# Weights of a two-block transformer kernel stored word by word in pairs of chunks, so that each weight load reads every second word

## The chip, the cores and the metric

The kernel runs on one core of a Trainium2 chip. The metric is device time in microseconds from the start to the end of one execution; the median of three runs stands for a kernel. Its engines are called by the names of the profile: PE (TensorE, its matmuls), PEld (TensorE's weight loads), DVE (VectorE), ACT (ScalarE), POOL (GpSimd) and SP (SyncE, which issues the transfers).

## The reference

Two transformer blocks of two layers each work on 256 latent tokens and 256 context tokens of width 1024, in float32. The first block has window attention, a Fourier mix and a short convolution between a wide input and an output projection; the second has three parts in each layer: a SwiGLU feed-forward, a mixer (differential attention with an mLSTM in layer 0, gated linear attention in layer 1) and another feed-forward. What matters here are the dense products with weights:

```python
y = gated_merge(a, ga, f, gf, s, gc, w_out)            # h @ w_out, 1024 x 1024, inputs by h @ w_in, 1024 x 2816
...
def swiglu(h, w_in, w_out):                            # 1024 x 5632 and 2816 x 1024, four pairs of them
    a, b = jnp.split(h @ w_in, 2, axis=-1)
    return (jax.nn.silu(a) * b) @ w_out
...
px = _split(hx @ w_in, EVEN_SPLITS)                    # mixers: 1024 x 3088, 1024 x 3104, and 1024 x 1024 out
```

## The kernel before

**Units and chunks.** A weight matrix is worked through in units of 1024 rows and 128 columns. Such a unit lies in SBUF as eight chunks `c` of 128 rows (the partitions) by 128 columns, one chunk behind the other: 1024 words of 4 bytes in each partition. An output projection of a feed-forward has units of six and five chunks.

**Split.** Float32 products are made of three products of a shorter format (`F32R`). Each unit that lands by DMA in `stage`, `wgate` or `deep` is split in two tiles of the same shape: `act_split` (L1467, on ACT) writes `w_hi`, a copy rounded to the short format, and `dve_split` (L1960, on DVE) writes `w_lo = unit - w_hi`. Both tiles have `RING` = 4 slots; the split of a unit waits until the unit four before it is used up (`unit_done`), and the feed runs `LEAD` = 3 units ahead of PE. The activations are split the same way into `h_hi`, `h_lo` (normed input) or `g_hi`, `g_lo` (the gated middle of a feed-forward).

**Matmul.** For each chunk, for each of the pairs (`w_hi`, `h_hi`), (`w_hi`, `h_lo`), (`w_lo`, `h_hi`) and for each 256 tokens there is one matmul: it loads a 128x128 chunk of a weight tile into the array as the stationary operand (the profile's LDWEIGHTS, PEld) and streams 256 words of activations (MATMUL, PE). So every matmul has a weight load of its own. Of `[:, u % RING, c, :]` the load takes 128 words that lie side by side. Most of this is in `pe_gemm` (L1118); the same form stands in the first GEMMs (L863), in `cross` and `head` (L962, L993) and in `seam`, the passage between a feed-forward and the next stage (L1035, L1065). In the names of the profile `ps<-h_hi,w_hi` the streamed tile stands first and the loaded one second.

**Token-major units.** The four short GEMMs with `evac="tok"` (V of the mixers, L1162) swap the roles: the activations are loaded and the weights `w_part[wp][:, u % RING:u % RING + 2, c, :]` are streamed.

**Order.** Every engine's program is written out by hand and tied by counting semaphores. Addresses are laid out by hand too: the tiles follow each other in the order of `sizes`, in which all but one are multiples of 8 KB in a partition (`vtok`, which lies ahead of the weights, has 64 bytes over), so `h_hi`, `h_lo`, `g_hi` and `g_lo` start at one place modulo 8 KB, and `w_hi` and `w_lo` 64 bytes further.

Of the kernel before, what the change touches and what calls it, by code (L numbers as in the profile page):

```python
# [16 lines left out]
P = 128  # L17
D = 1024
KC = D // P
SEQ = 256  # L20
# [330 lines left out]
def build_program(nc, t, const, out):  # L351
# [3 lines left out]
    with ExitStack() as stack:  # L355
# [189 lines left out]
        def arrival(u, i=0, turn=0):  # L545
# [11 lines left out]
            v = u - first_deep  # L557
            return deep[:, v % DEEP], deep_full[v % DEEP], i * (16 * turn // DEEP) + (16 * (v // DEEP) + 16), DEEP

        def splits(p, i, j, rounds):  # L560

            k = p.kw
            for s in range(k["per"]):
                x = j * k["per"] + s + LEAD + k.get("ahead", 0)
                if rounds > 1 or k["fed"] or i * k["step"] * k["per"] + x < k["n"] * k["per"]:
                    yield x
# [263 lines left out]
        def pe_first(eng, p):  # L830

            eng.wait_ge(S("s_ready"), 2)
            w_part, x_part = {"hi": w_hi, "lo": w_lo}, {"hi": h_hi, "lo": h_lo}

            def rows(n):
                eng.wait_ge(first_full[n], 16)
                if n >= 2:
                    eng.wait_ge(S("mod_sum"), n - 1)
                for k in range(KC):
                    j = k % 4  # L840
                    last = mm(ps[32 * j:32 * j + 32, 4 + n % 2, 0:SEG], svec[:, 0, k, 2:34], first_w[n][:, k, :], start=k < 4, stop=k >= 4)
                up(last, "mod_rows")

            def cols(n):
                eng.wait_ge(S("mod_sum"), n + 1)
                if n >= 2:
                    eng.wait_ge(S("mod_kept"), n - 1)
                for c in range(2):
                    last = tr(ps[:, 3 + 4 * (n % 2), c * P:(c + 1) * P], modr[:, n % 2, c * P:(c + 1) * P], ident)
                up(last, "mod_cols")  # L850

            def rstd(v):
                eng.wait_ge(S("diag_ready"), p.at("diag_ready", v - 1))
                up(mm(ps[:, 6, v * SEQ:(v + 1) * SEQ], onesPP, diag[:, v * SEQ:(v + 1) * SEQ], start=True, stop=True), "rstd_ready")

            def part(u, q):

                eng.wait_ge(S("w_ready"), u + 1)
                for c in (2 * q, 2 * q + 1):
                    eng.wait_ge(S("h_ready"), c + 1)  # L860
                    for wp, xp in W_X:
                        for v in range(0, NT, SEQ):
                            last = mm(ps[:, u, v:v + SEQ], w_part[wp][:, u % RING, c, :], x_part[xp][:, c, v:v + SEQ],  # L863
                                      start=c + v == 0 and wp == xp, stop=c == KC - 1 and wp == "lo", skip_group_check=True)
                if q == KC // 2 - 1:
                    up(last, "unit_done")

            for n in (4, 5):
                eng.wait_ge(S(f"bank_free{n}"), p.at(f"bank_free{n}"))
                rows(n - 4)  # L870
            evacuated(eng, p)
            cols(0)
            rstd(0)
            cols(1)
            rstd(1)
            rows(2)
            rows(3)
            cols(2)
            eng.wait_ge(S("consts_in"), 16 * CONST_LOADS)
            up(tr(ps[:, 2, 0:47], rows2[:, :], ident[0:47, 0:47]), "rows_T")  # L880
            cols(3)
            part(0, 0)
            rows(4)
            part(1, 0)
            cols(4)
            rows(5)
            part(0, 1)
            cols(5)
            part(1, 1)
            rows(6)  # L890
            cols(6)
            rows(7)
            part(0, 2)
            cols(7)
            for u, q in ((1, 2), (2, 0), (2, 1), (2, 2), (0, 3), (1, 3), (2, 3)):
                part(u, q)
            eng.wait_ge(S("mod_kept"), FIRST)
# [51 lines left out]
        def pe_cross(eng, p):  # L949

            u0 = p.at("unit_done")
            w_part, x_part = {"hi": w_hi, "lo": w_lo}, {"hi": h_hi, "lo": h_lo}
            for half in range(2):
                cols = slice(half * SEQ, (half + 1) * SEQ)
                for k in range(4):
                    if half == 0:
                        pe_rows(eng, p, 0, 4, k, 1)
                        eng.wait_ge(S("w_ready"), u0 + k + 1)
                    eng.wait_ge(S(f"bank_free{k}"), p.at(f"bank_free{k}", half))
                    for n, c in enumerate(OUT_ORDER):  # L960
                        for wp, xp in W_X:
                            last = mm(ps[:, k, cols], w_part[wp][:, (u0 + k) % RING, c, :], x_part[xp][:, c, cols],  # L962
                                      start=n == 0 and wp == xp, stop=n == KC - 1 and wp == "lo")
                        if half and (k, n) == (0, 3):
                            eng.wait_ge(S("mod_sum"), p.at("mod_sum", 2))
                            eng.wait_ge(S("mod_kept"), p.at("mod_kept", 2))
                            pe_post_sums(eng, p, 0, p.at("sq_used", 3), p.at("sq_ready", 4), 1)
                        if half and (k, n) == (1, 3):
                            pe_half_rstd(eng, p, 0, 1)
                    up(last, "unit_done" if half else "x_done")  # L970
                    if half == 0:
                        pe_cols(eng, p, 0, 4, k, 1)
            pe_pre_sums(eng, p, 0)
            pe_half_rstd(eng, p, 0, 2)
            pe_post_sums(eng, p, 1, p.at("sq_used", 6), p.at("sq_ready", 8), 3)

        def pe_head(eng, p):
# [3 lines left out]
            for half in (1, 0):  # L981
                cols = slice(half * SEQ, (half + 1) * SEQ)
                for q in range(2):
                    bank = 2 * q + 1 - half
                    eng.wait_ge(S(f"bank_free{bank}"), p.at(f"bank_free{bank}"))
                    if half:
                        eng.wait_ge(S("w_ready"), u0 + 2 * q + 2)
                    for n in range(KC):
                        if q == 0:
                            eng.wait_ge(S("h_ready"), p.at("h_ready", n + 1 - KC * half))  # L990
                        for j in range(2):
                            for wp, xp in W_X:
                                last = mm(ps[:, bank, j * SEQ:(j + 1) * SEQ], w_part[wp][:, (u0 + 2 * q + j) % RING, n, :], x_part[xp][:, n, cols],  # L993
                                          start=n + j == 0 and wp == xp, stop=n == KC - 1 and wp == "lo", skip_group_check=True)
                        if half and (q, n) == (0, 1):
                            for name in ("mod_sum", "mod_kept"):
                                eng.wait_ge(S(name), p.at(name))
                            pe_post_sums(eng, p, 0, p.at("sq_used"), p.at("sq_ready"), 1)
                        if half and (q, n) == (0, 4):
                            pe_half_rstd(eng, p, 0, 1)  # L1000
                    up(last, "c_done") if half else up(last, "unit_done", by=2)
# [4 lines left out]
        def pe_seam(eng, p):  # L1006
# [17 lines left out]
            for v in range(2):  # L1024
                cols = slice(v * SEQ, (v + 1) * SEQ)
                for j in range(2):
                    eng.wait_ge(S(f"bank_free{2 + j}"), p.at(f"bank_free{2 + j}", v))
                    for s, kc in enumerate(ks):
# [3 lines left out]
                        for n in range(kc):  # L1032
                            x = sum(ks[:s]) + n
                            for wp, xp in W_X:
                                last = mm(ps[:, 2 + j, cols], w_part[wp][:, u % RING, n, :], t_part[xp][:, x, cols],  # L1035
                                          start=x == 0 and wp == xp, stop=x == sum(ks) - 1 and wp == "lo")
                            if (v, j, x) == (0, 1, 6):
                                early_sums(0)
# [13 lines left out]
            for v in range(2):  # L1052
                cols = slice(v * SEQ, (v + 1) * SEQ)
                for q, n in (behind, () if k["latent"] else in_turn)[v]:
                    if q == 0:
                        eng.wait_ge(S("h_ready"), p.at("h_ready", KC * v + n + 1))
                    for j in range(2):
# [4 lines left out]
                                eng.wait_ge(S("w_ready"), u + 1)  # L1062
                            eng.wait_ge(S(f"bank_free{bank}"), p.at(f"bank_free{bank}", 2 * (bank // 2)))
                        for wp, xp in W_X:
                            last = mm(ps[:, bank, part], w_part[wp][:, u % RING, n, :], x_part[xp][:, n, cols],  # L1065
                                      start=n == 0 and wp == xp and (k["dst"] is not None or j == 0), stop=n == KC - 1 and wp == "lo", skip_group_check=True)
                        if n == KC - 1 and (v or k["latent"]) and k["dst"] is not None:
                            up(last, "unit_done")
# [29 lines left out]
        def pe_gemm(eng, p):  # L1098
# [16 lines left out]
            def chunk(j, u, c, x, first, final):  # L1115
                for wp, xp in W_X:
                    for v in range(a, b, SEQ):
                        last = mm(ps[:, j, v - a:v - a + SEQ], w_part[wp][:, u % RING, c, :], x_part[xp][:, x, v:v + SEQ],  # L1118
                                  start=first and wp == xp and v == a, stop=final and wp == "lo", skip_group_check=True)
                return last  # L1120

# [338 lines left out]
        def act_split(eng, u, i=0, turn=0, rounds=1):  # L1460
# [3 lines left out]
            if u >= RING:  # L1464

                eng.wait_ge(S("unit_done"), i * turn + (u - RING + 1))
            up(act(w_hi[:, u % RING], slot, ACT.Copy), "w_hi", rounds)  # L1467

        def act_feed(eng, p, units=range(LEAD)):
            for s in units:  # L1470
# [486 lines left out]
        def dve_split(eng, u, i=0, turn=0, rounds=1):  # L1957

            eng.wait_ge(S("w_hi"), i * turn + (u + 1))
            up(V.tensor_tensor(w_lo[:, u % RING], arrival(u)[0], w_hi[:, u % RING].bitcast(F32), ALU.subtract), "w_ready", rounds)  # L1960

        def dve_feed(eng, p, units=range(LEAD)):
            for s in units:
# [1267 lines left out]
```

## Time and profile before

| what | value |
|---|---|
| median of 3 runs | 2315.22 us (2311.31 to 2327.14) |
| profiled execution, span of its instructions | 2314.2 us |
| PE busy | 2227.1 us, 96% of the span, 19320 matmuls |
| PEld busy | 2091.2 us, 90% |
| DVE busy | 1145.4 us, 49% |
| ACT busy | 846.8 us, 37% |
| DMA queue that brings the weights | 46.1% of 16 engines' span |

No time outside the span is recorded for the profiled execution; its span is 1.0 us below the median of the runs, so the two are read as the same clock. A row of the profile gives for a group of equal instructions their number, the time in which at least one of them ran, and the mean duration of one. Matmuls overlap each other in the pipeline: the duration of one is longer than the time from its start to the next one's start. That second time, called spacing below, is read from the starts in the timeline, or from how many matmuls fall in a window. An entry of the timeline with `xN` covers N instructions; the spacing in it is its length, less the duration of one, divided by N - 1.

### The profile page before, as it was taken

The page shows a single profiled execution, that of the slowest core. Times are in us where ns is not written, and L with a number is a line of the kernel's source. Part 1 is how long each engine was busy: PE and PEld are TensorE (multiplying, and loading weights), DVE is VectorE, ACT ScalarE, POOL GpSimd, SP SyncE. Part 2 cuts the span into 40 slices and gives each one's busy share as a digit, 9 for nine tenths or more (in the row PEclk, how much of TensorE's full clock was granted, in tenths as well). Part 3 has the DMA queues.
Part 4 walks back from the last instruction along what each step waited for, and adds up shares of the span by engine and source line. Part 5 has one row for each costly group of instructions (what it writes and reads, how often), then busy time and mean ns, then how long its engine had stood idle before and what let it go on. Part 6 is the DMA issues. An engine that isn't in the chain of part 4 may idle for free. (4 is left out here: it accounts for less than half of the span.)

```text
span 2314.2 us, 46991 instructions
## 1 busy us (share of the span) xinstructions
PE 2227.1 (96%) x19320; PEld 2091.2 (90%) x19320; DVE 1145.4 (49%) x1930; ACT 846.8 (37%) x1384; POOL 176.3 (8%) x150
## 2 busy tenths in 40 slices
PE   6999999899999999998999999999999999999998
PEld 5986798799999999976999999999999998979998
DVE  5227375653433445456653333454343446487665
ACT  4226454632221233248432222243232234455444
POOL 0003112100000010501200000010000010001000
PEclk9999999999999999999999999999999999999999
DMA  9853544445676244520354666242233233225573
GB/s 297 234 167 86 172 133 104 128 147 154 186 216 186 86 131 117 149 80 28 102 175 141 190 207 189 84 126 85 81 114 94 86 96 101 74 82 146 168 202 112
DMA packets 515900, 315.76 MB, mean 136 GB/s; under 512 B 16035, under 2 KB 513274, under 8 KB 515622
## 3 DMA queue, kind: packets, MB, share of 16 engines
q1 hardware_dynamic: 515160, 313.45, 46.1%
q8 instruction: 113, 1.85, 0.3%
q14 instruction: 37, 0.30, 0.0%
q10 hardware_dynamic: 590, 0.16, 0.0%
HBM read 312.50 MB, written 1.06 MB: 135 GB/s over the span
## 5 line engine op out<-in xcount | busy, mean ns | idle before, releaser
L1118 PE MATMUL ps<-h_hi,w_hi 128*128 128x256 f32 x3376 | 728.0, 280 | 3.5 <-DVE h_lo L1726 1.7
L1118 PE MATMUL ps<-h_lo,w_hi 128*128 128x256 f32 x3376 | 720.6, 278 | 0.0
L1118 PE MATMUL ps<-h_hi,w_lo 128*128 128x256 f32 x3376 | 720.6, 278 | 0.0
L1118 PEld LDWEIGHTS ps<-h_hi,w_hi 128*128 128x128 f32 x3376 | 537.8, 189 | 22.9 <-issue 21.6
L1118 PEld LDWEIGHTS ps<-h_lo,w_hi 128*128 128x128 f32 x3376 | 539.4, 189 | 0.1
L1118 PEld LDWEIGHTS ps<-h_hi,w_lo 128*128 128x128 f32 x3376 | 537.9, 189 | 0.0
L1960 DVE TENSOR_TENSOR w_lo<-stage,w_hi 128x1024 fp32r<-128x1024 f32 x227 | 285.0, 1258 | 441.5 <-ACT w_hi L1467 440.9
L1467 ACT ACTIVATE w_hi<-stage 128x1024 fp32r<-128x1024 f32 x227 | 236.6, 1055 | 334.4 <-PE ps L1118 200.4
L1960 DVE TENSOR_TENSOR w_lo<-deep,w_hi 128x1024 fp32r<-128x1024 f32 x184 | 226.1, 1234 | 226.9 <-ACT w_hi L1467 225.2
L1467 ACT ACTIVATE w_hi<-deep 128x1024 fp32r<-128x1024 f32 x184 | 191.9, 1055 | 179.7 <-PE ps L1118 141.4
L1118 PE MATMUL ps<-g_hi,w_hi 128*128 128x256 f32 x1100 | 232.9, 280 | 0.2
L1118 PE MATMUL ps<-g_hi,w_lo 128*128 128x256 f32 x1100 | 231.7, 279 | 0.0
L1118 PE MATMUL ps<-g_lo,w_hi 128*128 128x256 f32 x1100 | 231.6, 279 | 0.0
L1519 ACT ACTIVATE vtok<-ps 128x512 f32<-128x512 f32 (+1 forms) x82 | 44.3, 540 | 472.5 <-PE ps L1118 472.4
L1118 PEld LDWEIGHTS ps<-g_hi,w_hi 128*128 128x128 f32 x1100 | 173.8, 188 | 4.2 <-issue 3.1
L1118 PEld LDWEIGHTS ps<-g_lo,w_hi 128*128 128x128 f32 x1100 | 174.0, 189 | 0.0
L1118 PEld LDWEIGHTS ps<-g_hi,w_lo 128*128 128x128 f32 x1100 | 173.6, 189 | 0.0
L2046 POOL MEMSET vtok<- 128x512 f32 x6 | 3.2, 526 | 1189.7 <-PE ps L1118 1189.7
L816 PE MATMUL ps<-modw,svec 128*32 128x256 f32 x1408 | 89.4, 386 | 0.0
L1989 DVE TENSOR_TENSOR vtok<-vtok,ps 128x512 f32<-128x512 f32 (+1 forms) x82 | 50.3, 613 | 76.6 <-PE ps L1118 76.6
L2002 DVE SCALAR_TENSOR_TENSOR resid<-ps,modA,resid 128x256 f32<-128x256 f32 (+1 forms) x120 | 53.4, 478 | 49.4 <-PE ps L1118 49.4
L1065 PE MATMUL ps<-h_hi,w_hi 128*128 128x256 f32 x224 | 65.4, 292 | 7.2 <-DVE h_lo L1864 4.2
(413 smaller groups left out, 2858.0 us busy)
## 6 DMA issues: line engine op xcount, KB each, us to landing
modw<-in_ada_w SPq DMA_DIRECT2D x72, 1024.0 KB, 6.7
stage<-in_ffn_w_in SPq DMA_DIRECT2D x88, 512.0 KB, 3.9
deep<-in_ffn_w_in SPq DMA_DIRECT2D x88, 512.0 KB, 3.9
modw<-in_w_mod SPq DMA_DIRECT2D x18, 1024.0 KB, 6.1
stage<-in_w_in SPq DMA_DIRECT2D x30, 512.0 KB, 5.3
stage<-in_ffn_w_out SPq DMA_DIRECT2D x32, 384.0 KB, 3.5
stage<-in_even_w_in SPq DMA_DIRECT2D x24, 512.0 KB, 4.0
deep<-in_ffn_w_out SPq DMA_DIRECT2D x32, 384.0 KB, 3.4
```

Source lines behind the costliest of these rows:

```text
L816: last = mm(ps[32 * j:32 * j + 32, 4, 0:SEG], svec[:, m["block"], k, lhs], modw[:, par, k, :], start=par == 0 and k < 4, stop=par == 1 and ...
L1065: last = mm(ps[:, bank, part], w_part[wp][:, u % RING, n, :], x_part[xp][:, n, cols], start=n == 0 and wp == xp and (k["dst"] is not None ...
L1118: last = mm(ps[:, j, v - a:v - a + SEQ], w_part[wp][:, u % RING, c, :], x_part[xp][:, x, v:v + SEQ], start=first and wp == xp and v == a, ...
L1467: up(act(w_hi[:, u % RING], slot, ACT.Copy), "w_hi", rounds)
L1519: up(act(sg[:, j // 2, 0:n], ps[:, j, 0:n], ACT.Silu), f"bank_free{j}", rounds)
L1960: up(V.tensor_tensor(w_lo[:, u % RING], arrival(u)[0], w_hi[:, u % RING].bitcast(F32), ALU.subtract), "w_ready", rounds)
L1989: up(V.tensor_tensor(gt[:, 0:n], sg[:, j // 2, 0:n], ps[:, j, 0:n], ALU.mult), f"bank_free{j}", rounds)
L2002: last = V.scalar_tensor_tensor(rs, ps[:, j, v * SEQ:(v + 1) * SEQ], gate[:, bass.ds(i * 8 + at, 1)], rs, ALU.mult, ALU.add)
L2046: up(nc.gpsimd.memset(sqsum[:, :], 0.0), "sums_clear")
```

## The change

For all units but the token-major ones the weight tiles keep their place and size, but the order of the words within a slot changes. Chunks 0 and 1 share the first 256 words of a slot: word 0 of chunk 0, word 0 of chunk 1, word 1 of chunk 0, and so on; then chunks 2 and 3, and so on. The load of a chunk thus takes 128 words at a step of two words, over 1024 bytes instead of 512. The number of loads, matmuls, splits, transfers and waits, and their order on every engine, stay what they were. The built access patterns of the three operations are, in words of 4 bytes (step and count, innermost last):

- load of a chunk: `[1, 128]` before, `[2, 128]` now
- `w_hi` written by the ACT split and `w_lo` written by the DVE split: `[1, 1024]` before, `[256, 4], [1, 2], [2, 128]` now; the unit from memory is read as `[1, 1024]` as before
- `w_hi` read by the DVE split: as the write

```diff
+        def woven(x):
+            return x.rearrange("p c n -> p (c n)").rearrange("p (d n s) -> p d s n", s=2, n=P)
+        def split_out(u, x):
+            return x if u in token_units else woven(x)
+        def split_in(u, x):
+            return x if u in token_units else x.rearrange("p (d s) n -> p d s n", s=2)
+        def stationary(part, slot, c):
+            return woven(part[:, slot])[:, c // 2, c % 2, :]
...
-                        last = mm(ps[:, j, v - a:v - a + SEQ], w_part[wp][:, u % RING, c, :], x_part[xp][:, x, v:v + SEQ],
+                        last = mm(ps[:, j, v - a:v - a + SEQ], stationary(w_part[wp], u % RING, c), x_part[xp][:, x, v:v + SEQ],
...
-            up(act(w_hi[:, u % RING], slot, ACT.Copy), "w_hi", rounds)
+            up(act(split_out(u, w_hi[:, u % RING]), split_in(u, slot), ACT.Copy), "w_hi", rounds)
...
-            up(V.tensor_tensor(w_lo[:, u % RING], arrival(u)[0], w_hi[:, u % RING].bitcast(F32), ALU.subtract), "w_ready", rounds)
+            up(V.tensor_tensor(split_out(u, w_lo[:, u % RING]), split_in(u, arrival(u)[0]), split_out(u, w_hi[:, u % RING].bitcast(F32)), ALU.subtract), "w_ready", rounds)
```

The same replacement of `w_part[wp][:, slot, c, :]` by `stationary(...)` is made at L863, L962, L993, L1035 and L1065. `token_units` are the units of the four token-major GEMMs.

## Rows read from the trace of the kernel before

**Rows 1.** Page, part 1: engine, busy us, share of the span, instructions.
```profile
PE 2227.1 (96%) x19320; PEld 2091.2 (90%) x19320; DVE 1145.4 (49%) x1930; ACT 846.8 (37%) x1384; POOL 176.3 (8%) x150
```

**Rows 2.** Groups by form: loads of a weight chunk; busy us, mean ns; idle before.
```profile
L1118 PEld LDWEIGHTS ps<-h_hi,w_hi 128*128 128x128 f32 x3376 | 537.8, 189 | 22.9 <-issue 21.6 <-DVE w_lo L1960 0.9 <-DVE h_lo L1767 0.4
...
L1118 PEld LDWEIGHTS ps<-g_hi,w_hi 128*128 128x128 f32 x1100 | 173.8, 188 | 4.2 <-issue 3.1 <-DVE w_lo L1960 0.8 <-ACT vtok L1519 0.2
...
L1065 PEld LDWEIGHTS ps<-h_hi,w_hi 128*128 128x128 f32 x224 | 43.0, 192 | 10.1 <-DVE h_lo L1864 5.5 <-issue 4.6
...
L863 PEld LDWEIGHTS ps<-h_hi,w_hi 128*128 128x128 f32 x48 | 7.2, 188 | 6.1 <-issue 5.6 <-DVE w_lo L1960 0.4
```

**Rows 3.** Windows, L1118 alone: stretch and its us; PE busy (matmuls); PEld busy (loads); clock; DMA.
```profile
1680.00:1740.00 60.00, 60.00 (x532) 60.00 (x532) 1.00 0.41 120
...
2120.00:2180.00 60.00, 60.00 (x511) 60.00 (x511) 1.00 0.61 175
...
700.00:715.00 15.00, 15.00 (x135) 15.00 (x134) 1.00 0.59 183
```

**Rows 4.** Timeline of PE in cross (L962), two stretches 2 us apart.
```profile
291.16 0.28 PE L962 MATMUL ps<-h_lo,w_hi 128*128 128x256 f32 x1
...
291.96 0.28 PE L962 MATMUL ps<-h_hi,w_lo 128*128 128x256 f32 x1
...
293.31 0.28 PE L962 MATMUL ps<-h_hi,w_hi 128*128 128x256 f32 x1
...
295.67 0.28 PE L962 MATMUL ps<-h_hi,w_lo 128*128 128x256 f32 x1
```

**Rows 5.** Timeline of PEld: loads of 128 words behind short matmuls.
```profile
303.91 1.42 PEld L924 LDWEIGHTS ps<-ones,vtok 128*128 128x128 f32 x12
...
1048.12 0.97 PEld L2522 LDWEIGHTS ps<-vda,scr 128*128 128x128 f32 x8
```

**Rows 6.** Timeline of PE: sixteen transposes of 128 columns in a row.
```profile
385.54 1.91 PE L2192 MATMUL ps<-cst,big 128*128 128x128 f32 x16
```

**Rows 7.** Groups by form: loads of 32 and 64 words.
```profile
L816 PEld LDWEIGHTS ps<-modw,svec 128*32 128x32 f32 x1408 | 39.7, 110 | 29.4 <-issue 6.2
...
L2253 PEld LDWEIGHTS ps<-vtok 128*64 128x64 f32 x160 | 8.5, 136 | 2.0 <-issue 1.0 <-ACT vtok L2321 1.0
```

**Rows 8.** One line, L2239, loads one word 64 times; ns min/median/max, first and last start.
```profile
L2239 PEld LDWEIGHTS ps<-cst,small x96: 132/137/137, 216.6 to 425.8; 128*64 128x64 f32 x96
```

**Rows 9.** One line, L2482: 512 streamed words behind loads of 128 and of 64 words.
```profile
L2482 PEld LDWEIGHTS ps<-h_hi,wgate_hi x8: 187/187/188, 987.2 to 991.9; 128*128 128x128 f32 x8
L2482 PE MATMUL ps<-h_hi,wgate_hi x8: 389/389/392, 987.4 to 992.1; 128*128 128x512 f32 x8
...
L2482 PE MATMUL ps<-h_hi,wlr_hi x8: 388/396/399, 1949.3 to 1954.2; 128*64 128x512 f32 x8
```

**Rows 10.** Groups by form: matmul of L1118, and the two splits.
```profile
L1118 PE MATMUL ps<-h_hi,w_hi 128*128 128x256 f32 x3376 | 728.0, 280 | 3.5 <-DVE h_lo L1726 1.7 <-ACT big L1525 1.2 <-DVE big L1881 0.3
...
L1960 DVE TENSOR_TENSOR w_lo<-deep,w_hi 128x1024 fp32r<-128x1024 f32 x184 | 226.1, 1234 | 226.9 <-ACT w_hi L1467 225.2
L1467 ACT ACTIVATE w_hi<-deep 128x1024 fp32r<-128x1024 f32 x184 | 191.9, 1055 | 179.7 <-PE ps L1118 141.4 <-PE ps L1162 23.9 <-DVE small L3074 5.7
```

**Rows 11.** Windows, last feed-forward: stretch; busy of PE, PEld, DVE, ACT, POOL; clock; DMA.
```profile
2112.20:2300.60 188.40, 188.38 (x1587) 188.40 (x1587) 123.23 (x168) 90.53 (x111) 5.71 (x8) 0.99 0.57 165
```

**Rows 12.** Groups of that stretch: the splits.
```profile
L1960 DVE TENSOR_TENSOR w_lo<-deep,w_hi 128x1024 fp32r<-128x1024 f32 x73 | 88.7, 1223 | 51.9 <-ACT w_hi L1467 50.9
L1467 ACT ACTIVATE w_hi<-deep 128x1024 fp32r<-128x1024 f32 x73 | 76.3, 1054 | 44.1 <-PE ps L1118 44.1
```

**Rows 13.** Timeline of DVE in that stretch, its output projection.
```profile
2206.62 1.23 DVE L1960 TENSOR_TENSOR w_lo<-deep,w_hi 128x1024 fp32r<-128x1024 f32 x1 [0.90 <-ACT w_hi L1467]
2207.77 0.48 DVE L2002 SCALAR_TENSOR_TENSOR resid<-ps,modA,resid 128x256 f32 x1
2208.47 1.23 DVE L1960 TENSOR_TENSOR w_lo<-deep,w_hi 128x1024 fp32r<-128x1024 f32 x1 [0.23 <-ACT w_hi L1467]
```

More of the change, by code:

```diff
@@ L558, in arrival @@
             return deep[:, v % DEEP], deep_full[v % DEEP], i * (16 * turn // DEEP) + (16 * (v // DEEP) + 16), DEEP
+        token_units = {u for q in phases if q.kind == "gemm" and q.kw["evac"] == "tok"
+                       for u in range(q.at("unit_done"), q.at("unit_done") + 2 * q.kw["n"])}
+        def woven(x):
[6 more added lines that the diff above has]
+            return woven(part[:, slot])[:, c // 2, c % 2, :]
         def splits(p, i, j, rounds):
@@ L862, in part @@
                         for v in range(0, NT, SEQ):
-                            last = mm(ps[:, u, v:v + SEQ], w_part[wp][:, u % RING, c, :], x_part[xp][:, c, v:v + SEQ],
+                            last = mm(ps[:, u, v:v + SEQ], stationary(w_part[wp], u % RING, c), x_part[xp][:, c, v:v + SEQ],
                                       start=c + v == 0 and wp == xp, stop=c == KC - 1 and wp == "lo", skip_group_check=True)
@@ L961, in pe_cross @@
                         for wp, xp in W_X:
-                            last = mm(ps[:, k, cols], w_part[wp][:, (u0 + k) % RING, c, :], x_part[xp][:, c, cols],
+                            last = mm(ps[:, k, cols], stationary(w_part[wp], (u0 + k) % RING, c), x_part[xp][:, c, cols],
                                       start=n == 0 and wp == xp, stop=n == KC - 1 and wp == "lo")
@@ L992, in pe_head @@
                             for wp, xp in W_X:
-                                last = mm(ps[:, bank, j * SEQ:(j + 1) * SEQ], w_part[wp][:, (u0 + 2 * q + j) % RING, n, :], x_part[xp][:, n, cols],
+                                last = mm(ps[:, bank, j * SEQ:(j + 1) * SEQ], stationary(w_part[wp], (u0 + 2 * q + j) % RING, n), x_part[xp][:, n, cols],
                                           start=n + j == 0 and wp == xp, stop=n == KC - 1 and wp == "lo", skip_group_check=True)
@@ L1034, in pe_seam @@
                             for wp, xp in W_X:
-                                last = mm(ps[:, 2 + j, cols], w_part[wp][:, u % RING, n, :], t_part[xp][:, x, cols],
+                                last = mm(ps[:, 2 + j, cols], stationary(w_part[wp], u % RING, n), t_part[xp][:, x, cols],
                                           start=x == 0 and wp == xp, stop=x == sum(ks) - 1 and wp == "lo")
@@ L1064, in pe_seam @@
                         for wp, xp in W_X:
-                            last = mm(ps[:, bank, part], w_part[wp][:, u % RING, n, :], x_part[xp][:, n, cols],
+                            last = mm(ps[:, bank, part], stationary(w_part[wp], u % RING, n), x_part[xp][:, n, cols],
                                       start=n == 0 and wp == xp and (k["dst"] is not None or j == 0), stop=n == KC - 1 and wp == "lo", skip_group_check=True)
```

## The prediction

> **What bounds the kernel now.** I read the page first: PE is busy 96% of the span and DVE 49%, ACT 37% [rows 1], so a change can only move the time through PE, or by making another engine hold PE up. Then I asked for the groups by form. Almost all matmuls have one shape: a load of 128 weight words and 256 streamed words. The loads with `w_hi` or `w_lo` in them come in eight groups of three products, from L1118 with 3376 and 1100 to L863 with 48 (between these two ends 224, 132, 64, 64 and 32): 5040, times three products 15,120 matmuls [rows 2]. They are the loads that the change touches. They hardly wait: ahead of the 3376 loads of the first group PEld sat idle 22.9 us, 0.9 us of it for a split [rows 2]. So the time of these stretches is number times spacing.
>
> The spacing is the number to look at. In windows of L1118 it has two levels. Between 1680 and 1740 us 532 matmuls fall in 60 us, between 2120 and 2180 us 511; one or two of each count only reach in from the edge, so that is 113 and 118 ns [rows 3]. Counting all starts of L1118 in the timeline, 8793 steps are of 112 to 114 ns and 4383 of 115 to 119 ns, mean 114.8. The level doesn't follow the data's place: in one phase, on the same line and with the same tiles, eight matmuls from 291.16 to 291.96 us are 0.80/7 = 114 ns apart, and two microseconds on, twenty steps from 293.31 to 295.67 us give 118 ns [rows 4]. Nor does it follow the other traffic: it is 15/133 = 113 ns at 183 GB/s of transfers and the same at 120 GB/s [rows 3]. A level lasts until PE is next held up, then it is drawn anew. That is how two streams look that run beside each other in step.
>
> **What each stream needs alone.** A load of 32 words takes 110 ns, one of 64 words 136, one of 128 words 188: 26/32 = 0.81 and 52/64 = 0.81 ns a word, behind some 84 ns of latency [rows 2, 7]. So 128 words need 104 to 107 ns. Where the matmuls behind loads of 128 words are short, the loads set the spacing: (1.42 - 0.19)/11 = 112 ns at L924, (0.97 - 0.19)/7 = 111 ns at L2522 [rows 5]. Where a streamed operand of the same length in time as ours sets it (transposes, L2192), it is (1.91 - 0.27)/15 = 109 ns [rows 6]. So our 113 ns stand 1 to 2 ns above the floor of the loads, and 4 ns above that of the streaming; the 118 ns stand 6 and 9 above. Load and stream are almost equally late, and whatever the change does to a load shows at once: **one nanosecond of spacing is 15,120 x 1 ns = 15 us, 0.65% of the time**.
>
> **The change part by part.**
>
> Loads, number and order: unchanged, 0 us.
>
> Loads, their rate. No load in the trace has a step of two words, so the bounds are from afar. Below: the spacing can't fall under the 109 ns of the stream, (114.8 - 109) x 15,120 = -88 us. Above: if every second-word fetch cost the load a beat more for each word, 128 x 0.81 = 104 ns come on top and the spacing is 113 + 104 = 217 ns: +1545 us. Which end is nearer? Two rows speak against the upper one. A load that takes one word 64 times over takes 137 ns [rows 8], as the 136 of a load of 64 neighbours [rows 7]: the load is paced by its columns, not by how many words a fetch brings. And the streamed operand moves through 256 neighbouring words, 1024 bytes, in 113 ns without harm; the woven load moves through the same 1024 bytes in the same time, so TensorE already reads at this rate on one of its two sides.
>
> Why it may gain. Today the stream walks 4 bytes each 0.42 ns (256 words in 107 ns) and the load 4 bytes each 0.81 ns, so in every matmul the stream passes the load by 512 bytes. If the two can get in each other's way at some addresses, they must meet several times in each matmul, and how often depends on how they started: two levels. The 512-word matmuls of L2482 hint that way. With 128 words loaded they last 389 ns, with 64 words from another tile 396 [rows 9]; both should be the same if only the stream counted, and fewer loaded words cost more. In the woven order both walk 8 bytes each 0.83 ns, side by side. If they collide at all, one is held for a beat and from then on they no longer do. Then the spacing falls to what the load alone allows, 112 ns [rows 5]: (114.8 - 112) x 15,120 = **-42 us**. I take this value and not the 109, since the loads of 128 words show 111 to 112 wherever they are the later.
>
> The Trainium skill speaks against this reading: "TensorE: Matmul & The Clock Gate", in its section on the steps of a matmul, says that the two operands have read ports of their own and that loading the next weights takes no read bandwidth from the running matmul. By that the two levels have another cause and the change gives 0 us here. The trace, with two levels for the same instructions, doesn't bear it out fully; it is the second case below.
>
> Splits. 412 ACT copies and 412 DVE subtractions write (and DVE also reads `w_hi`) at a step of two words; today they take 1.06 and 1.23 us [rows 10]. No row shows such a step. Below, nothing is gained: 0 us, they aren't what PE waits for. Above I take twice the duration. What covers them: they run up to three units ahead, and DVE is half idle [rows 1]. A unit over 512 tokens lasts 48 x 115 = 5.5 us, far above 2.5. The cover is thin where only 256 tokens are left, most of all in the last feed-forward: DVE is busy 123.2 of 188.4 us [rows 11], 88.7 of them in 73 splits [rows 12]. Doubled, that is 212 us of work for 188: +24 us there, and I put half as much on the shorter stretches with 256 tokens, +36 us in all. With a split longer by two thirds, 2.0 us, the feed-forward as a whole would still hold (182 of 188), but in its output projection, where splits start 1.85 us apart and an update of 0.48 us stands between them [rows 13], DVE needs about 2.0 + 0.24 a unit for 1.95: 32 units x 0.3 = +10 us. ACT has 90.5 + 76 = 167 of 188 even when doubled, and holds. I take +3 us: most units have the 5.5 us of cover, and for the others I allow some tenths of a microsecond.
>
> The Trainium skill has two rules here that differ. "Advanced Engine Details and Errata" (Memory Cachelines) gives lines of 16 bytes and asks for two hits on each, which a step of two float32 words keeps: +0 us for load and split. "Vector Engine (DVE) Microarchitecture Reference" (Measured stream behaviour on trn2) asks DVE for runs of two neighbouring words; by that the woven side of a split is the slow case, some 1.7 to 2 times as long, and the sum is that of the upper bounds above. No run here shows either yet.
>
> Sum: 2314.2 - 42 + 3 = 2275, against the span; the median of the runs is 1 us above it, so 2275 us stands, 1.7% below.
>
> **The rivals.**
>
> *Nothing happens* (28%). Load and stream don't meet, the load is as quick with a step of two, the splits are covered. The levels are still drawn anew: all at 113 would be -(114.8 - 113.3) x 15,120 = -22 us, all at 118 +45 us; a third at the slow level as now gives 2315 us.
>
> *The load pays a little per fetch* (17%), the case that ends slower. The load covers twice the bytes, so if it loses some time at each border (its 112 ns hold 5 ns above 107), that share doubles. Its own spacing is then 112 + 5 = 117, and where it sits beside the stream with 2 to 3 ns more, 120 ns: (120 - 114.8) x 15,120 = +79 us, 2394 us. The point from which it decides is 113 ns: below it the load is still hidden, and each ns above costs 15 us. For it speaks how near the load is to binding [rows 5]; against it, that the fetch doesn't pace a load [rows 7, 8].
>
> *The load pays a beat per word* (9%): 217 ns, 2314 + 1545 = 3860 us. The mechanism is one fetch of neighbouring pairs per two words, of which the woven load uses half. The rule on pairs in the Trainium skill's "Vector Engine (DVE) Microarchitecture Reference" (Measured stream behaviour on trn2) would say this, carried from DVE to TensorE; the loads of 64 words [rows 7, 8] don't bear it out, since one word taken again is as quick as neighbours.
>
> *DVE becomes the bound* (6%): load and stream unchanged, splits twice as long, 2314 + 36 = 2350 us, decided in the last feed-forward at a split of about 2.1 us.
>
> *The gain* (40%) at 2275 us, between 2228 (stream alone, 109 ns) and 2290.
>
> **How the numbers follow.** A measurement of this kernel can tell about 1% from no change. Of the gain's 40% I put 2 within 1%: faster 0.38. These 2 and the 28% without effect make 0.30 for the same. Slower is 17 + 9 + 6 = 0.32. The range reaches from the stream's floor, 2228, to the load that pays per fetch, 2395. It leaves out the 9% of the doubled load and some 8% beyond both ends. The likeliest case's own range is 2228 to 2290.
>
> **What would show it.** The gain: windows of L1118 with some 535 matmuls in 60 us everywhere, one level instead of two, the last feed-forward at 178 us instead of 188. The load that pays: fewer than 505 in 60 us, PEld's mean duration above 192 ns, also at its shortest. No effect: both levels again, in another mix. The splits: mean of the two groups on L1979 and L1486 of the new file, and idle time of PEld before loads that waits for `w_lo`. I am wrong altogether if the levels come from something that a load's addresses don't touch, or if a step of two is slow for TensorE alone.

## The result, and the profile after

The changed kernel takes 2395.11 us in the median of four runs (2391.29 to 2397.28), the kernel before 2315.2 us beside it. The ratio of the runs is 1.0329, with a 95% interval from 1.0301 to 1.0357: slower by 3.3%, 80 us. The profiled execution has a span of 2395.5 us against 2314.2, and its own time is 1.8 us above its span.

First the page of the changed kernel, part 1, then the groups by form that answer to [rows 2] and [rows 10]: busy us, mean ns of one, idle time before.

```profile
PE 2311.7 (97%) x19320; PEld 2173.9 (91%) x19320; DVE 1145.3 (48%) x1930; ACT 885.7 (37%) x1384; POOL 176.5 (7%) x150
```

```profile
L1137 PE MATMUL ps<-h_hi,w_hi 128*128 128x256 f32 x3376 | 743.7, 285 | 3.7 <-DVE h_lo L1745 1.7 <-ACT big L1544 1.2 <-DVE big L1900 0.3
...
L1137 PEld LDWEIGHTS ps<-h_hi,w_hi 128*128 128x128 f32 x3376 | 561.3, 195 | 23.4 <-issue 21.8 <-DVE w_lo L1979 1.3 <-DVE h_lo L1786 0.2
...
L1979 DVE TENSOR_TENSOR w_lo<-deep,w_hi 128x1024 fp32r<-128x1024 f32 x184 | 225.6, 1231 | 247.4 <-ACT w_hi L1486 247.1
L1486 ACT ACTIVATE w_hi<-deep 128x1024 fp32r<-128x1024 f32 x184 | 209.2, 1150 | 182.4 <-PE ps L1137 143.8 <-PE ps L1181 23.8 <-DVE small L3093 5.7
...
L1181 PEld LDWEIGHTS ps<-w_hi,h_hi 128*128 128x128 f32 x256 | 48.0, 188 | 0.5 <-issue 0.3 <-ACT big L1544 0.2
```

The line to read is the second: a load now lasts 195 ns instead of 189, while its idle time is what it was (23.4 us instead of 22.9, 1.3 of it for a split). The last line is a control in the same profile: in the token-major units the load takes activations, which weren't rearranged, and lasts 188 ns as ever. DVE's split didn't change (1231 ns, before 1234), ACT's copy took on 0.1 us (1150 ns, before 1055), and PE hardly waits for it.

Then the windows that answer to [rows 3]: stretch, PE busy with matmuls of this line, PEld with loads, clock, DMA.

```profile
1740.00:1800.00 60.00, 60.00 (x503) 60.00 (x502) 1.00 0.37 109
2220.00:2280.00 60.00, 60.00 (x503) 60.00 (x502) 1.00 0.57 167
700.00:715.00 15.00, 15.00 (x128) 15.00 (x127) 1.00 0.67 206
```

Less one or two at the edges that is 119.5 to 119.8 ns in both long windows, and 15/126 = 119 in the short one. Over the whole span the starts of L1137 give a mean of 120.02 ns; 4326 steps are of 115 to 119 ns, 8880 of 120 to 124, and a single one lies between 112 and 114 ns, where two thirds lay before. (120.02 - 114.84) x 15,120 = 78 us of the 81 us by which the spans differ. So all but some 3 us of the loss lies in the spacing. The question is what of the change makes it, and by which rule.

### The profile page after: what moved, and what is told of

It is laid out like the page before. It is cut to its first block, busy times and chain, and to the rows that moved or that the text cites. A ratio compares the mean times of both kernels' runs of the same rounds, so it can differ in the third digit from the quotient of the medians.

```text
span 2395.5 us, 46991 instructions
## 1 busy us (share of the span) xinstructions
PE 2311.7 (97%) x19320; PEld 2173.9 (91%) x19320; DVE 1145.3 (48%) x1930; ACT 885.7 (37%) x1384; POOL 176.5 (7%) x150
## 3 DMA queue, kind: packets, MB, share of 16 engines
HBM read 312.50 MB, written 1.06 MB: 131 GB/s over the span
## 4 chain that ended last, share of the span: by engine, by line
PE 90%; DVE 6%; ACT 2%; issue 1%; DMA 1%; SPq 0%; POOL 0%; DVEq 0%; ACTq 0%; POOLq 0%
PE ps L1137 68%; PE ps L1181 4%; PE ps L835 3%; PE ps L1084 3%; PE ps L1054 2%; DVE w_lo L1979 1%; PE ps L1012 1%; PE ps L882 1%; PE ps L2233 1%; PE ps L2249 1%; PE ps L981 1%; PE ps L943 1%; PE ps L2272 1%; PE ps L2597 1%; ACT w_hi L1486 1%
## 5 line engine op out<-in xcount | busy, mean ns | idle before, releaser
L1137 PE MATMUL ps<-h_hi,w_hi 128*128 128x256 f32 x3376 | 743.7, 285 | 3.7 <-DVE h_lo L1745 1.7
L1137 PE MATMUL ps<-h_lo,w_hi 128*128 128x256 f32 x3376 | 740.2, 283 | 0.0
L1137 PE MATMUL ps<-h_hi,w_lo 128*128 128x256 f32 x3376 | 737.6, 283 | 0.0
L1137 PEld LDWEIGHTS ps<-h_hi,w_hi 128*128 128x128 f32 x3376 | 561.3, 195 | 23.4 <-issue 21.8
L1137 PEld LDWEIGHTS ps<-h_hi,w_lo 128*128 128x128 f32 x3376 | 558.8, 195 | 0.0
L1137 PEld LDWEIGHTS ps<-h_lo,w_hi 128*128 128x128 f32 x3376 | 557.6, 195 | 0.0
L1979 DVE TENSOR_TENSOR w_lo<-stage,w_hi 128x1024 fp32r<-128x1024 f32 x227 | 284.0, 1253 | 460.9 <-ACT w_hi L1486 460.4
L1486 ACT ACTIVATE w_hi<-stage 128x1024 fp32r<-128x1024 f32 x227 | 258.7, 1153 | 337.8 <-PE ps L1137 212.5
L1979 DVE TENSOR_TENSOR w_lo<-deep,w_hi 128x1024 fp32r<-128x1024 f32 x184 | 225.6, 1231 | 247.4 <-ACT w_hi L1486 247.1
L1486 ACT ACTIVATE w_hi<-deep 128x1024 fp32r<-128x1024 f32 x184 | 209.2, 1150 | 182.4 <-PE ps L1137 143.8
L1137 PE MATMUL ps<-g_lo,w_hi 128*128 128x256 f32 x1100 | 235.8, 282 | 0.0
L1137 PE MATMUL ps<-g_hi,w_lo 128*128 128x256 f32 x1100 | 235.7, 282 | 0.0
L1137 PE MATMUL ps<-g_hi,w_hi 128*128 128x256 f32 x1100 | 235.6, 282 | 0.1
L1137 PEld LDWEIGHTS ps<-g_hi,w_hi 128*128 128x128 f32 x1100 | 180.0, 194 | 4.0 <-issue 3.4
L1137 PEld LDWEIGHTS ps<-g_lo,w_hi 128*128 128x128 f32 x1100 | 179.1, 194 | 0.0
L1137 PEld LDWEIGHTS ps<-g_hi,w_lo 128*128 128x128 f32 x1100 | 178.6, 194 | 0.0
L1084 PE MATMUL ps<-h_hi,w_hi 128*128 128x256 f32 x224 | 66.0, 295 | 7.3 <-DVE h_lo L1883 3.8
```

Source lines behind the costliest of these rows:

```text
L1084: last = mm(ps[:, bank, part], stationary(w_part[wp], u % RING, n), x_part[xp][:, n, cols], start=n == 0 and wp == xp and (k["dst"] is not ...
L1137: last = mm(ps[:, j, v - a:v - a + SEQ], stationary(w_part[wp], u % RING, c), x_part[xp][:, x, v:v + SEQ], start=first and wp == xp and v ...
L1486: up(act(split_out(u, w_hi[:, u % RING]), split_in(u, slot), ACT.Copy), "w_hi", rounds)
L1979: up(V.tensor_tensor(split_out(u, w_lo[:, u % RING]), split_in(u, arrival(u)[0]), split_out(u, w_hi[:, u % RING].bitcast(F32)), ALU.subtra ...
```

## The experiments

**Loads alone and splits alone.** The edit of the first leaves the splits as before the change, that of the second the loads:

```diff
 # loads_only
         def split_out(u, x):
-            return x if u in token_units else woven(x)
+            return x
         def split_in(u, x):
-            return x if u in token_units else x.rearrange("p (d s) n -> p d s n", s=2)
+            return x
 # splits_only
         def stationary(part, slot, c):
-            return woven(part[:, slot])[:, c // 2, c % 2, :]
+            return part[:, slot, c, :]
```

Loads alone, expected: 

> The loads take every second word, but both splits write their tiles as in the kernel before, so the chunks that are multiplied are not those of the matrices. Theory L (the load itself is slower over 1024 bytes): all of the loss is here, 2395 us within 5, spacing of L1137 120 ns, duration of a load 194 to 195 ns. Theory S (the splits' writes at a step of two delay the feed): 2315 us, and the loads at 188 ns.

Splits alone, expected: 

> The splits write the woven order, but the loads take 128 neighbouring words as before, so again the chunks that are multiplied are mixtures. Theory L: 2315 us within 10 (the two levels of spacing may be drawn in another mix), loads at 188 ns; ACT's split at 1.15 us as in the changed kernel. Theory S: 2395 us.

Measured: loads alone 2391.9 us (2391.36 to 2392.92), ratio 1.0343 (1.0317 to 1.0369); splits alone 2316.7 us, ratio 1.0009 (0.9993 to 1.0026). The groups of the two kernels, loads alone first:

```profile
L1137 PEld LDWEIGHTS ps<-h_hi,w_hi 128*128 128x128 f32 x3376 | 559.8, 195 | 23.6 <-issue 22.3 <-DVE w_lo L1979 1.2
...
L1486 ACT ACTIVATE w_hi<-stage 128x1024 fp32r<-128x1024 f32 x227 | 236.6, 1055 | 346.1 <-PE ps L1137 219.9 <-DMA stage<-in_ffn_w_out 40.9 <-PE ps L1181 34.4
```

```profile
L1137 PEld LDWEIGHTS ps<-h_hi,w_hi 128*128 128x128 f32 x3376 | 538.6, 189 | 23.7 <-issue 22.0 <-DVE w_lo L1979 1.5
...
L1979 DVE TENSOR_TENSOR w_lo<-stage,w_hi 128x1024 fp32r<-128x1024 f32 x227 | 284.1, 1254 | 449.2 <-ACT w_hi L1486 448.7
L1486 ACT ACTIVATE w_hi<-stage 128x1024 fp32r<-128x1024 f32 x227 | 256.5, 1145 | 326.0 <-PE ps L1137 186.3 <-DMA stage<-in_ffn_w_out 47.4 <-PE ps L1181 34.9
```

The load's 195 ns and the whole loss go with the loads; ACT's 1145 ns go with the splits and cost nothing that can be measured. Theory S fell.

**A load at a step of four.** On top of the loads-only edit:

```diff
         def stationary(part, slot, c):
-            return woven(part[:, slot])[:, c // 2, c % 2, :]
+            return part[:, slot].rearrange("p c n -> p (c n)").rearrange("p (d n s) -> p d s n", s=4, n=P)[:, c // 4, c % 4, :]
```

Expected: 

> Splits as in the kernel before, loads at a step of four words over 2048 bytes (other words than the matrices need). Theory L1 (a load pays for each further stretch of bytes that it crosses, 6.7 ns for each 512 bytes): duration 188 + 3 x 6.7 = 208 ns, spacing 134 ns, 2315 + 15,120 x 19 ns = 2600 us. Theory L2 (any step but one costs the same once): duration 195 ns, spacing 120 ns, 2395 us. Theory L3 (lines of 16 bytes, free as long as two words of a line are used, dear when only one is): far slower than both, spacing over 200 ns, 3600 us or more.

Measured in one run: 4096.2 us. Its group of loads:

```profile
L1137 PEld LDWEIGHTS ps<-h_hi,w_hi 128*128 128x128 f32 x3376 | 987.3, 331 | 21.9 <-issue 21.3 <-DVE w_lo L1979 0.4
```

The load lasts 331 ns and the spacing is 234.6 ns on average. Theories L1 (2600 us) and L2 (2395 us) fell, and L3 held but for its word "free": a step of two is only nearly so. The step from one word to two costs 6 ns, the step from two to four 136. That is no price per byte. It looks as if four words came together, and a load that uses two of them was almost as quick as one that uses all.

**Load and stream by themselves.** A small kernel runs bursts of 40 equal matmuls, each pair of load and stream on a line of its own, such as:

```python
# load step 2
bursts(lambda i: mm(o(i, 256, P), w(0, 2, 128), x(0, 1, 256), start=True, stop=True, skip_group_check=True))
# load step 2, stream one word
bursts(lambda i: mm(o(i, 256, P), w(0, 2, 128), x(0, 0, 256), start=True, stop=True, skip_group_check=True))
```

`w(at, step, n)` is the loaded operand, `x(at, step, n)` the streamed one; a step of 0 takes one word again and again. The tiles stand 64 bytes apart modulo 8 KB, as in the full kernel.

Expected: 

> A kernel by itself, which leaves all of the reference's work out and copies x to the output. It runs four bursts of 40 equal matmuls for each of 30 pairs of load and stream, each pair on a line of its own, in the kernel's short format unless said. Collision theory (load and stream get in each other's way): with 256 streamed words and a load at a step of one 113 or 118 ns; when the stream takes one word only, or the load one word only, 109 to 112 ns. Theory of separate costs (each side pays for its own fetches): the load's duration is 188 ns at a step of one, 195 at two, 208 at four, 235 at eight and about 181 with one word taken 128 times, whatever the stream; the stream's spacing at 512 words is 227 ns whatever the load, and 216 when it takes one word only. Float32 with 64 streamed words, where the load alone sets the spacing: 112 ns at a step of one, 118 at two, 132 at four by the theory of bytes.

Its timeline on PE, one burst of each line (start, length of the burst, matmuls). L98: steps 1 and 1, L100: load at 2, L104: 3, L106: 4, L108: 8, L110: one word loaded 128 times. L112: load at 1 while one word is streamed, L114: load at 2 with that. L118: load at 1, stream at 2, L120: stream in pairs of neighbours, every second pair, L124: stream at 4. L136, L138: stream from word 8 and 16. L150, L152: float32, load at 1 and 2, 64 streamed words; each of their matmuls counts twice.

```profile
19.21 4.81 PE L98 MATMUL ps<-xs,ws 128*128 128x256 f32 x40 [0.20 <-DVE pad L79]
...
39.52 5.08 PE L100 MATMUL ps<-xs,ws 128*128 128x256 f32 x40 [0.20 <-DVE pad L79]
...
83.92 7.21 PE L104 MATMUL ps<-xs,ws 128*128 128x256 f32 x40 [0.20 <-DVE pad L79]
...
115.96 9.61 PE L106 MATMUL ps<-xs,ws 128*128 128x256 f32 x40 [0.20 <-DVE pad L79]
...
155.58 10.00 PE L108 MATMUL ps<-xs,ws 128*128 128x256 f32 x40 [0.20 <-DVE pad L79]
...
191.23 5.07 PE L110 MATMUL ps<-xs,ws 128*128 128x256 f32 x40 [0.20 <-DVE pad L79]
...
211.72 4.74 PE L112 MATMUL ps<-xs,ws 128*128 128x256 f32 x40 [0.20 <-DVE pad L79]
...
231.72 4.98 PE L114 MATMUL ps<-xs,ws 128*128 128x256 f32 x40 [0.20 <-DVE pad L79]
...
276.65 9.42 PE L118 MATMUL ps<-xs,ws 128*128 128x256 f32 x40 [0.20 <-DVE pad L79]
...
315.13 9.42 PE L120 MATMUL ps<-xs,ws 128*128 128x256 f32 x40 [0.20 <-DVE pad L79]
...
392.36 9.57 PE L124 MATMUL ps<-xs,ws 128*128 128x256 f32 x40 [0.20 <-DVE pad L79]
...
530.49 4.99 PE L136 MATMUL ps<-xs,ws 128*128 128x256 f32 x40 [0.20 <-DVE pad L79]
...
551.33 5.05 PE L138 MATMUL ps<-xs,ws 128*128 128x256 f32 x40 [0.20 <-DVE pad L79]
...
768.84 9.14 PE L150 MATMUL ps<-xf,wf 128*128 128x64 f32 x80 [0.20 <-DVE pad L79]
...
806.70 9.64 PE L152 MATMUL ps<-xf,wf 128*128 128x64 f32 x80 [0.20 <-DVE pad L79]
```

The first matmuls of a burst are further apart, so the length of a burst gives some 3 ns more than its settled part: (4.81 - 0.28)/39 = 116 ns for L98, where the second half stands at 113.3. The spacing in the second half of a burst, with the pieces of 16 bytes that a load touches:

| load at step | pieces of 16 bytes | spacing, stream of 256 words | spacing, one word streamed |
|---|---|---|---|
| 1 | 32 | 113.3 ns | 112.0 ns |
| 2 | 64 | 120.1 | 117.8 |
| 3 | 96 | 173.3 | |
| 4 | 128 | 233.3 | |
| 8 | 128 | 244.0 | |

With one word streamed the load is the later of the two (512 words of such a stream take 218.7 ns in L146, so 256 need 109), and it needs 112.0 ns at a step of one and 117.8 ns at a step of two. The float32 lines say the same: 111.7 and 117.8 ns, at full granted clock. This is the floor that the changed kernel met. The steps of four and eight touch equally many pieces and cost nearly the same, 5% apart, though one crosses twice the bytes; from two to three and from three to four 32 pieces more cost 53 and 60 ns, 1.7 to 1.9 ns a piece. A load that goes by its words (0.81 ns each, 104 ns) is overtaken by its pieces once 64 x 1.8 = 115 ns are due. That this is a fetch of 16 bytes is my reading of these numbers. "Advanced Engine Details and Errata" in the Trainium skill (Memory Cachelines) gives lines of 16 bytes, with full performance from two hits on each; for a load the traces agree with the size and with a single hit being dear, but two hits are 5% short of full speed.

Two float32 lines add to this, since the granted clock fell from 2.4 to 1.2 GHz while PE was in one of their bursts: L154 here (load at a step of four) and L141 of the next kernel (a step of three). First the two pieces of L154 before and after the fall, then those of L141:

```profile
836.21 3.48 PE L154 MATMUL ps<-xf,wf 128*128 128x64 f32 x14 [0.20 <-DVE pad L79]
...
841.63 10.71 PE L154 MATMUL ps<-xf,wf 128*128 128x64 f32 x45
```

```profile
347.14 2.94 PE L141 MATMUL ps<-xf,wf 128*128 128x64 f32 x16
...
351.77 6.61 PE L141 MATMUL ps<-xf,wf 128*128 128x64 f32 x30
```

At a step of four the settled spacing is 233.3 ns at either clock. At a step of three it is 173.3 ns at 2.4 GHz, as in L104, and 213.3 ns at 1.2 GHz, which is also what one word loaded 128 times needs there (L156; 111.7 ns at 2.4 GHz in the next kernel). So in these lines a load takes the longer of two times: one for its words, which doubles when the clock halves, and one for the pieces that it touches, which doesn't follow the clock.

The collision theory's other half came out mixed. One streamed word instead of 256 brings 113.3 down to 112.0 and no further, as the load alone needs that. With one word loaded over and over (L110) the bursts were 113.3, 120.0, 113.3 and 120.0 ns: two levels with the same code and place. With the load started at word 1 or word 16 they were 118.3 and 118.7. So the place matters, which the next kernel asks. The theory of separate costs was right for the load at steps of one and two (188, 194 ns) and wrong elsewhere: at steps of four and eight the loads lasted 329 and 340 ns where it said 208 and 235, and a stream of 512 words was not at 227 ns whatever the load but at 233.3 beside neighbours, 231.4 to 231.7 beside one word and 230.0 beside a load at a step of two. There, with the stream the later by far, the woven load does disturb it less, by 3.3 ns; with 256 words its own 117.8 ns outweigh that.

**Where the load starts.** The same kernel with other lines, bursts of 30, the load starting at another word of its tile: `w(o, 1, 128)` for 35 values of `o`.

Expected: 

> A kernel by itself, which leaves all of the reference's work out and copies x to the output; four bursts of 30 equal matmuls for each pair of load and stream, 256 streamed words, each pair on a line of its own. The load starts at words 0, 4, 8 to 124 and 128, 192, 256 of its tile, the stream always at word 0 of its own. Theory A (the level of the spacing is set by the place of the load against that of the stream): the four bursts of a line agree within 0.5 ns, the lines differ between 113 and 120 ns, and repeat after 64 or 128 words. Theory H (the level is drawn at each start): the bursts of one line fall on both levels. With the load at a step of two: no offset below 117.5 ns, since the load alone needs that; 117.5 to 120.5. Float32 loads with 64 streamed words at full clock: at a step of three 128 words over 96 lines of 16 bytes, by the rule of 1.77 ns a line 170 plus 5, 175 ns; with one word taken 128 times 107 to 112 ns.

Its timeline: L101, L135, L169: load from words 0, 64, 128, one or two of the four bursts of each; L103, L109, L133: from words 4, 16 and 60; L175, L179: at a step of two from words 0 and 4.

```profile
17.27 3.80 PE L101 MATMUL ps<-xs,ws 128*128 128x256 f32 x30 [0.20 <-DVE pad L82]
...
25.28 3.69 PE L101 MATMUL ps<-xs,ws 128*128 128x256 f32 x30 [0.20 <-DVE pad L82]
...
33.19 3.82 PE L103 MATMUL ps<-xs,ws 128*128 128x256 f32 x30 [0.20 <-DVE pad L82]
...
81.51 3.82 PE L109 MATMUL ps<-xs,ws 128*128 128x256 f32 x30 [0.20 <-DVE pad L82]
...
286.72 3.94 PE L133 MATMUL ps<-xs,ws 128*128 128x256 f32 x30 [0.20 <-DVE pad L82]
...
299.02 3.69 PE L135 MATMUL ps<-xs,ws 128*128 128x256 f32 x30 [0.20 <-DVE pad L82]
302.90 3.80 PE L135 MATMUL ps<-xs,ws 128*128 128x256 f32 x30 [0.20 <-DVE pad L82]
...
622.88 3.69 PE L169 MATMUL ps<-xs,ws 128*128 128x256 f32 x30 [0.20 <-DVE pad L82]
...
662.17 3.88 PE L175 MATMUL ps<-xs,ws 128*128 128x256 f32 x30 [0.20 <-DVE pad L82]
...
694.71 3.84 PE L179 MATMUL ps<-xs,ws 128*128 128x256 f32 x30 [0.20 <-DVE pad L82]
```

Both theories hold a part. The spacing depends on where the load starts, and repeats every 64 words: word 4 gives 118.6 to 118.7 ns and word 68 118.5 to 118.8, word 20 and word 84 both 119.9 to 120.0, word 40 and word 104 both 116.6 to 116.9. What counts is the place against the stream: moving the stream instead, from word 0 to 8 or 16 (L136 and L138 of the first small kernel), gives 118.3 and 120.0 ns, as the load does from words 56 and 48, which lie as far from a stream at word 0, modulo 64. Of the places tried only 0, 64, 128, 192 and 256 ever reach 113.3 ns, and at the first four of them each burst falls on 113.3 or on 117.8: there the level is set at the start. It isn't set by chance alone, since the four bursts of words 64 and 128 take the two levels in the same order. Other places have two levels too, words 60 and 124 those of 117.8 and 122.9 ns, again in the same order. At a step of two every place lies between 118.6 and 121.9, word 4 lowest. Of the two float32 lines of this kernel, one word taken 128 times needs 111.7 ns, the same as 128 neighbours, at the high end of what was expected; the load at a step of three, expected at 175 ns, is the L141 above with 173.3.

**Places in the full kernel.** A gap ahead of the weight tiles moves them, with the order of their words as it was before the change (`"gap": 16` and `"gap": 64` words ahead of `"scr"` in `sizes`). It moves the tiles behind them too, `modw` with the landing place `deep`, `wfbd` and `svec`. (The last two aren't multiples of 8 KB either, which my account of the map left out; they stand behind the weights and don't shift them.) In the changed kernel both weight tiles are made four words longer and used from word 4 on, and `scr` is 8 words longer:

```diff
 # before_64B, before_256B with 64
-                 "scr": 2 * RING * KC * P,
+                 "gap": 16, "scr": 2 * RING * KC * P,
 # after_16B, and the same for w_lo
-        w_hi = over("w_hi", "scr", 0, [P, RING, KC, P], F32R)
+        w_hi = over("w_hi", "scr", 0, [P, RING * KC * P + 4], F32R)[:, 4:].rearrange("p (r c n) -> p r c n", r=RING, c=KC)
```

64 bytes further, expected: 

> The kernel before, with the weight tiles 64 bytes further, so that they start 128 bytes instead of 64 from the place of the activations modulo 256. Theory A (the place of the load against that of the stream decides how often they meet): the 113 ns level is gone, spacing 118.7 ns as in the small kernel at word 16, 2315 + 15,120 x 3.9 ns = 2373 us. Theory 0 (addresses don't matter in the full kernel): 2315 us with both levels.

256 bytes further, expected: 

> The kernel before, with the weight tiles 256 bytes further, which by the small kernel is the same place again (words 0, 64, 128). Theory A: 2315 us, within 1%, the same two levels near 113 and 118 ns. Theory 0: the same. A theory that some other distance counts (512 or 1024 bytes): spacing 117 ns or more and over 2340 us.

The woven kernel 16 bytes further, expected: 

> The changed kernel, with the weight tiles 16 bytes further, the best place of the small kernel for loads at a step of two (118.7 ns at word 4, 120.0 at word 0). Theory A: 1.3 ns less spacing, 2395 - 20 = 2375 us. Theory 0: 2395 us. By both it stays slower than the kernel before, since such a load alone needs 117.8 ns.

| kernel | time | ratio to before (95%) | mean spacing |
|---|---|---|---|
| before, 64 bytes further | 2376.82 us | 1.0245 (1.0218 to 1.0271) | 118.68 ns |
| before, 256 bytes further | 2317.19 us | 1.0005 (0.9987 to 1.0022) | 114.20 ns |
| changed, 16 bytes further | 2375.35 us | 1.0237 (1.0204 to 1.0269) | 118.75 ns |

Windows of L1118 in the kernel before with 64 bytes of gap, and of L1137 in the woven one with 16:

```profile
1740.00:1800.00 60.00, 60.00 (x508) 60.00 (x507) 1.00 0.36 104
```

```profile
1740.00:1800.00 60.00, 60.00 (x502) 60.00 (x502) 1.00 0.35 101
2220.00:2280.00 60.00, 60.00 (x508) 60.00 (x508) 1.00 0.65 182
```

The small kernel's numbers carry over to a tenth of a nanosecond (118.7 at word 16, 118.7 for the woven load at word 4), and the three times came within 4 us of what was expected from them. The kernel before stands at the one of sixteen tried places modulo 256 bytes that reaches 113 ns; no kernel that was tried beats it. The woven load, wherever it stands, can't: it needs 117.8 ns alone.

## Why the prediction was wrong

**The point, 2275 us, was wrong, and its step was the rate of the load.** I let the spacing fall "to what the load alone allows, 112 ns" and took this 112 from loads of neighbours. The term stood at -42 us, and it measured about +80. A load at a step of two alone needs 117.8 ns, in the short format with one word streamed and in float32 alike. With that number in the sum every version of the gain is gone, since 117.8 is above the 114.8 of before.

**Two rows were read for more than they hold.** That one word loaded 64 times is no quicker than 64 neighbours [rows 7, 8] shows that fewer fetches don't help; it says nothing of more fetches. And the argument that TensorE reads 1024 bytes in a matmul on its streaming side without harm carried a row from one side to the other, which the runs don't allow: a step of two words costs a load 5% (112.0 to 117.8 ns) and doubles the time of a stream (L118). Reckoned backwards, 113 ns for the 64 pieces of the stream is 1.77 ns a piece, near the 1.8 of a load, but that likeness is no rule: a stream at a step of four touches 256 pieces in 233.3 ns (L124), 0.91 ns each. No row of the kernel before gave the price; it took the small kernel.

**The rival "the load pays a little per fetch" is what happened**, at 17%. Its signs came, 503 matmuls in 60 us and loads of 195 ns. It gave 120 ns and 2394 us; measured are 120.02 ns and 2395.11 us, a tenth of a microsecond beyond the upper end of the range. Its price was set by another path (the 5 ns above 107 doubled, and 2 to 3 ns beside the stream); the runs put 5.8 ns on the load alone (117.8 against 112.0) and 2.2 ns on the stream beside it (120.0 against 117.8). A loss for each stretch of bytes crossed would have given 107 + 3 x 5 = 122 ns at a step of three and 127 at four, and they took 173.3 and 233.3. So its mechanism was only near the true one, and that its sum came so close was luck in part. The 15 us for each nanosecond hold: 3.8 ns gave 60 us in the kernel moved by 64 bytes, 120 ns gave 1780 us at a step of four.

**Load and stream do get in each other's way**, and here the page that speaks of read ports of their own is not the whole story for this format: in "TensorE: Matmul & The Clock Gate" (Step-by-step: what each phase is for), the Trainium skill says that loading takes no read bandwidth from the running matmul, yet moving the weights by 64 bytes costs 2.5%. But the weave doesn't settle the meeting as I thought. Beside the stream of 256 words the woven load loses 1 to 4 ns at every place tried. And the hint from the 512-word matmuls [rows 9] compared two places and not only two lengths: the tile of the 64-word loads lies 64 bytes from the activations modulo 256, that of the 128-word loads 0 bytes. In the small kernel, both at 64 bytes, 128 words give 233.3 ns and 64 words 231.0 to 232.7 (L140, L148).

**"The level doesn't follow the data's place" was half true.** At the kernel's place two levels exist, and a start sets which, as I read from [rows 4]; elsewhere modulo 256 bytes there are other levels and never 113 ns. "Drawn anew" says too much: in the kernel before, the three long stretches of L1118 from 800, 1492 and 1860 us are all at 117.8 ns.

**The splits** were sized at 0 to 36 us and put at 3. DVE reads and writes at a step of two in the same time (1253 ns against 1258); the rule on pairs of neighbours, from "Vector Engine (DVE) Microarchitecture Reference" (Measured stream behaviour on trn2) in the Trainium skill, would have made them 1.7 to 2 times as long, and isn't borne out for a step of two words. ACT's copy is 0.1 us longer. Splits alone: ratio 1.0009, interval across 1.

**The load that pays a beat per word** (9%) was about the right size for a step of four: 4096 us and 234.6 ns, where it gave 3860 and 217. **Wholly unaffected loads** (28%) fell with the 195 ns.

What stays open: why the meeting of load and stream repeats every 256 bytes, why a stream's time doesn't follow its pieces of 16 bytes as a load's does, and what at a start decides between 113 and 118 ns at the kernel's place. Whoever could set it would gain up to (114.84 - 113.3) x 15,120 = 23 us, 1%; none of these kernels tried to.

## What to carry to other kernels

Where every matmul has a load of its own, compare the two spacings first, each alone: if load and stream lie within a few nanoseconds, the layout of the loaded operand is on the path, and every layout of the load that touched more pieces of 16 bytes lost, from 5% at twice as many to double at four times. A row bounds a cost on one side only: before leaning on it, ask whether the thing measured there does more or less of what the change adds. And the place of the weights against the activations, modulo 256 bytes, is a tuning knob worth 2.5% here, which any edit of the memory map turns unnoticed.

## What the hardware showed that I had not expected

- A streamed operand at a step of two words costs double at once: 229.3 ns for 256 words instead of 113.3 (L118), no less when it takes pairs of neighbours (L120) and hardly more at a step of four (233.3 ns, L124), while a load at a step of two costs 5% (112.0 to 117.8 ns).
- A load at a step of four words needs 233.3 ns at a granted clock of 2.4 GHz and of 1.2 GHz alike, while one word loaded 128 times goes from 111.7 to 213.3 ns.
- The spacing of equal matmuls depends on where the load starts against the stream, from 113.3 to 122.9 ns, with a period of 64 words.
- In one kernel and at one place the spacing has two levels, 113.3 and 117.8 ns, that last until the next stop of PE.
- DVE is indifferent to a step of two words on one source and on its output; ACT writes 1024 words so in 1.15 us instead of 1.06.
